# The last expert pair with its down-projection between two halves of an up-projection, and two of the last eight weight transfers issued as sixteen of eight rows

## The reference

```python
logits = jnp.dot(x2, w_router) + b_router        # 320 tokens, 32 experts
top_v, top_e = lax.top_k(logits, TOP_K)          # 4 experts for each token
gate = jax.nn.softmax(top_v, axis=-1)
# for each expert e and its tokens x:
u = x @ w1[e] + b1[e]                            # 1024 -> 2048
x_glu = jnp.minimum(u[..., ::2], 7.0)
x_lin = jnp.clip(u[..., 1::2], -7.0, 7.0)
y = (x_glu * sigmoid(1.702 * x_glu) * (x_lin + 1.0)) @ w2[e] + b2[e]   # 1024 -> 1024
out = h + sum over the token's 4 experts of gate * y
```

## Time and profile before

| | |
|---|---|
| median of 3 runs | 1192.15 us (1191.0 to 1194.05) |
| profiled execution | 1192.19 us |
| its span, first to last instruction | 1190.1 us |
| TensorE clock granted | 0.994 of full speed |
| PE busy | 1149.8 us (97%) |
| DVE, ACT, POOL busy | 367.2, 177.5, 28.9 us |
| DMA | 440.03 MB, 370 GB/s over the span; from 600 us on 423 to 436 in every slice of 30 us but the last |

### The profile page before, as it was taken

One profiled execution on the slowest core, in us unless ns is written; L12 is line 12 of the kernel. 1 busy time (PEld: TensorE's weight loads), 2 busy tenths in 40 slices (PEclk: granted clock), 3 DMA queues, 4 the chain that ended last, 5 costly groups with the idle time before them and its releaser, 6 DMA issues.

```text
span 1190.1 us, 14238 instructions
## 1 busy us (share of the span) xinstructions
PE 1149.8 (97%) x6178; PEld 568.7 (48%) x6178; DVE 367.2 (31%) x759; ACT 177.5 (15%) x327; POOL 28.9 (2%) x54
## 2 busy tenths in 40 slices
PE   8999999999999999999999999999899999999998
PEld 7679988645434343434344343434343434343433
DVE  3637876423312221222223222212121212121222
ACT  2225233022101010111011010101010101010111
POOL 3220000000000000000000000000000000000000
PEclk9999999999999999999999999999999999999999
DMA  9433248967999899999999999999999999999996
GB/s 302 145 90 118 90 150 277 409 256 304 420 425 428 353 439 423 438 425 436 426 435 428 433 429 432 432 427 435 426 436 427 434 429 433 428 433 423 427 428 262
DMA packets 46977, 440.03 MB, mean 370 GB/s; under 512 B 3902, under 2 KB 21664, under 8 KB 29872
## 3 DMA queue, kind: packets, MB, share of 16 engines
q1 hardware_dynamic: 44768, 434.19, 88.0%
q0 software_dynamic: 1904, 4.10, 1.2%
q10 hardware_dynamic: 240, 0.79, 0.2%
HBM read 436.38 MB, written 3.67 MB: 370 GB/s over the span
## 4 chain that ended last, share of the span: by engine, by line
PE 61%; DMA 31%; DVE 4%; ACT 2%; issue 2%; ACTq 0%; DVEq 0%
DMA ring<-in_w 31%; PE ps L1254 22%; PE ps L1312 13%; PE ps L1334 4%; PE ps L793 3%; PE ps L1020 3%; PE ps L1042 2%; PE ps L1119 2%; PE ps L760 2%; PE ps L750 1%; PE ps L727 1%; PE ps L1269 1%; ACT xnT L1692 1%; DMA acc<-in_x_sample 1%; PE ps L1281 1%
## 5 line engine op out<-in xcount | busy, mean ns | idle before, releaser
L1254 PE MATMUL ps<-ring,hnT 128*64 128x512 f32 x2032 | 448.4, 598 | 13.4 <-DMA ring<-in_w 12.7
L1254 PEld LDWEIGHTS ps<-ring,hnT 128*64 128x64 f32 x2032 | 143.6, 138 | 302.2 <-issue 280.7
L1312 PE MATMUL ps<-ring,xnT 128*64 128x512 f32 x992 | 220.8, 597 | 13.8 <-DMA ring<-in_w 13.8
L2226 DVE TENSOR_TENSOR xnT<-ps,b1T 128x512 f32<-128x512 f32 x32 | 22.1, 692 | 448.1 <-PE ps L1269 448.1
L1312 PEld LDWEIGHTS ps<-ring,xnT 128*64 128x64 f32 x992 | 74.9, 138 | 155.3 <-issue 152.4
L1679 ACT COPY hnT<-ps 128x1024 f32<-128x1024 f32 x32 | 32.4, 1012 | 511.9 <-PE ps L1254 511.9
L2247 DVE TENSOR_TENSOR acc<-acc,ps 128x1024 f32<-128x1024 f32 x30 | 36.5, 1218 | 205.0 <-PE ps L1334 187.4
L1334 PE MATMUL ps<-xnT,cst 128*128 128x512 f32 (+1 forms) x180 | 76.0, 619 | 1.6
L1119 PE MATMUL ps<-cst,region 128*128 128x128 f32 x512 | 61.9, 278 | 0.7 <-issue 0.7
L1119 PEld LDWEIGHTS ps<-cst,region 128*128 128x128 f32 x512 | 58.5, 192 | 2.8 <-issue 0.9
L1691 ACT COPY xnT<-ps 64x512 f32<-64x512 f32 x31 | 17.9, 579 | 243.1 <-PE ps L1312 243.1
(11 more groups left out here) (311 smaller groups left out, 840.6 us busy)
## 6 DMA issues: line engine op xcount, KB each, us to landing
ring<-in_w SPq DMA_DIRECT2D x71, 4096.0 KB, 39.1
ring<-in_w SPq DMA_DIRECT2D x33, 2048.0 KB, 26.5
ring<-in_w SPq DMA_DIRECT2D x28, 1024.0 KB, 10.3
ring<-in_w_in SPq DMA_DIRECT2D x17, 1024.0 KB, 5.3
ring<-in_w_o SPq DMA_DIRECT2D x2, 2048.0 KB, 11.7
ring<-in_w SPq DMA_DIRECT2D x8, 512.0 KB, 22.5
ring<-in_w_b SPq DMA_DIRECT2D x1, 2048.0 KB, 11.7
ring<-in_w_a SPq DMA_DIRECT2D x4, 512.0 KB, 6.4
```

The source lines that it names most:

```text
L1254: mm = pe.matmul(ps[o:o + 64, bank + q // 2, into].rearrange("p (j x) -> p j x", x=4), stationary, columns[:, q], start=(at == 0), stop=(a ...
L1312: mm = pe.matmul(ps[64 * c:64 * c + 64, 6, :], hT[:, which, order_of(f), :], ring[:, slot, D * (f % 2) + 512 * c:D * (f % 2) + 512 * c + 512],
L2226: dve.tensor_tensor(glu, ps[:, 2, :].rearrange("p (f t) -> p f t", f=KF), wide(b1T[:, bass.ds(e, 1), 0, :].rearrange("p a f -> p (a f)").u ...
```

## The change

The chunk list of the last pair, PE's order, and ACT's order of two copies are changed together: w1(30) first half, w2(29), w1(30) second half. Transfers 4 and 5 (counted from 0) of the last eight become sixteen each, of eight rows; the same semaphores then count to 256.

```diff
+END_PARTS = [1, 1, 1, 1, 16, 16, 1, 1]
+
 CHUNKS = []
 for _p in range(EXPERTS // 2):
-    CHUNKS += [("w1", 2 * _p, h) for h in range(2)]
-    if _p:
-        CHUNKS += [("w2", 2 * _p - 1, 0)]
+    _up = [("w1", 2 * _p, h) for h in range(2)]
+    if _p == EXPERTS // 2 - 1:
+        CHUNKS += [_up[0], ("w2", 2 * _p - 1, 0), _up[1]]
+    else:
+        CHUNKS += _up + [("w2", 2 * _p - 1, 0)] * (_p > 0)
     CHUNKS += [("w1", 2 * _p + 1, h) for h in range(2)] + [("w2", 2 * _p, 0)]
 CHUNKS += [("w2", EXPERTS - 1, 0)]
...
             def load_end(m, c):
                 for i in range(2):
                     for j in range(2):
-                        sp.dma_start(ring[:, m + i, 1024 * j:1024 * j + 1024].rearrange("p (k c) -> p k c", k=2),
-                                     w2_end[c, i, j]).then_inc(w2_last[4 * c + 2 * i + j], 16)
+                        dst = ring[:, m + i, 1024 * j:1024 * j + 1024].rearrange("p (k c) -> p k c", k=2)
+                        rows_ = P // END_PARTS[4 * c + 2 * i + j]
+                        for r in range(0, P, rows_):
+                            sp.dma_start(dst[r:r + rows_], w2_end[c, i, j][r:r + rows_]).then_inc(w2_last[4 * c + 2 * i + j], 16)
...
                     if f % 2 == 0:
-                        pe.wait_ge(w2_last[4 * c + f // 2], 16 if main else 16 * loads + 16)
+                        n = 16 * END_PARTS[4 * c + f // 2]
+                        pe.wait_ge(w2_last[4 * c + f // 2], n if main else n * loads + n)
...
             def last_body(p, again=None, loads=None, b=None):
                 main = again is None
 
-                up(2 * p, 0, again)
+                up(2 * p, 0, again, steps=range(4))
                 down(2 * p - 1, 1, loads)
+                up(2 * p, 0, again, steps=range(4, KD))
                 turn(2 * p)
...
             def last_body(p):
+                copy_y(2 * p - 1, 1, 3 * p)
                 copy_u(2 * p)
-                copy_y(2 * p - 1, 1, 3 * p)
                 gate_sigmoid(2 * p)
```

## The result

The changed kernel took 1199.46 us (median of four, 1198.41 to 1200.29) against 1192.09 for the one before, measured beside it: a ratio of 1.006, 95% interval 1.0034 to 1.0086. That is +7.4 us; +6.0 was forecast, and the range held it. The profiled execution took 1198.81, its span is 1196.7, so the span grew by 6.6. Where these 6.6 us lie can be read to a tenth. The times compared in this document are of fast executions: one execution of the stepped eight-row kernel took 1482.33 us at a mean granted clock of 0.75, and that kernel's ratio leaves it out.

A forecast was written before the change was run, and what follows sets the result against it. TensorE, busy 97% of the span, was taken as the bound; late issue put the sixth piece at 1183.6 instead of 1177.64, swallowing the order's +1.2: 1192.15 + 6.0 = 1198.2 us, range 1192.6 to 1204.

The forecast's parts named there:

- Part 1: New order of chunks, loads and PE: up's result copy stands bare before the transposes, so up(31) starts 1.2 us later.
- the wait that was to stay: PE's wait for a weight load ending at 1140.36, expected unchanged, now ahead of the last quarter of up(30).
- The +0.4 for this part alone: At the end, the new order alone costs +0.4 us: of its +1.2, small waits for loads absorb the rest.
- Issue: SP issuing 32 small transfers at 0.59 us each: last issued at 1181.5, sixth piece landed at 1183.6.
- Engines: Eight-row transfers use eight engines, so pieces land 2.6 us apart, the sixth at 1180.2, hidden behind 1183.6.
- rival A: In the last loads, issue is cheap and eight engines bind: +2.6, 1194.8 us; 22% together with issues up to 0.5.
- rival B: In the last loads, the partitions' outlet binds, four engines at each: sixth piece at 1194.6, +17, 1209 us; 15%.
- B's objection: Against outlet crowding in the last loads: some engines finish some 5 us ahead, and those on different row blocks don't meet.
- All behind moves as it is: After the wait for the sixth piece, remaining work and stores only shift, by the +6.0 us.
- The sum: PE goes on with the sixth piece at 1183.6 instead of 1177.64, +6.0: 1192.15 + 6.0 = 1198.2 us.
- Its sign that PE goes on before 1181: In the last down-projection: the forecast is wrong if PE goes on with the sixth piece before 1181.
- Rival C: Small transfers hidden on early engines, all issued from 1157.5 on; PE goes on at 1178.0: +0.4, 1192.6 us; 16%.

The follow-up runs named there:

- experiment 1: The new order alone, the eight last transfers whole as in the kernel before: 1192.43 us, ratio 1.0009 to the kernel before.
- e4_rows16: The changed kernel with transfers 4 and 5 as eight transfers of sixteen neighbouring rows each: 1196.28 us, ratio 1.0033 to the kernel before.
- the three fillers: The changed kernel plus three matmuls whose result is never read, ahead of the sixth piece's wait: 1199.51 us, ratio 1.0059 to the kernel before.

## Why the prediction was right, and where it was not

**Part 1: right up to up(31), mis-sized behind it.** The bare copy, the transposes at 1145.2, up(31) at 1152.4 and its disappearance in the wait are all in the trace. One detail differs: PE reached the last part of up(30) later than before, so the wait that was to stay is not in the changed kernel's trace (in that of the order alone it is, 0.96 us); the bare copy began at 1144.17 all the same. The +0.4 for this part alone took idle time of weight loads for time that PE loses: the trace of the order alone has +1.1, as worked out under experiment 1. It cost the forecast nothing, since the longer wait for the sixth piece swallows either.

**Issue: the term was mis-sized, and it isn't the one that binds.** 0.59 us per small transfer came from a single row of ACT's queue. Eight neighbouring rows take 0.30 on SP, one each 0.34 us, and the sixth piece was all issued by about 1175.0, not 1181.5. The queue was read only roughly: the sum had 5.7 of the sixteen out by 1166.6, one each 1.6 us, and the trace has none before 1164.5 and then seven by 1166.6. The runs with stepped rows show that the price exists on SP for another shape, 0.59 with a step. Why the row on ACT had it, with eight neighbouring partitions and no step, no run shows.

**Engines: the reason named as hidden is where the time went.** By the prediction's own sign, issues under 0.46, this is rival A, whose sum was 1175.0 + 2 x 2.6 = 1180.2. Measured is 1177.2 + 5.4 = 1182.6. Its second term is near in size; its first is the step that failed: the fourth piece was taken as untouched. The sixteen engines are not in step. The semaphores of the pieces count an engine's completions, and the traces have the times: those of the fourth piece came from 1168.3 to 1175.0 before, and from 1167.7 to 1177.2 after. With sixteen rows to a transfer (e4_rows16) the first completions of the fifth piece came at 1168.2, while the last of the fourth came at 1177.6. So early engines are already at the small transfers while late ones still carry the whole pieces, and packets are slower just there (87 to 122 ns). That this is rival B's crowding at the outlet of the partitions, at a price of a few microseconds in place of its 17, fits the 64-row kernel and the earlier trace rows but is argued, not shown: no trace tells which engine writes where, and the two kernels with spread rows disagree. B's objection, that engines out of step don't meet, was at most half right; its sign, a wait for the fifth piece as well, is there (0.72).

The engines behind the 5.4 are not settled either: with 64 rows on sixteen engines it is 1182.23 - 1177.37 = 4.9 already (the latter is where PE went on with the fourth piece there), with 32 rows 4.4 (1179.96 - 1175.58). Only the last step, fifth to sixth, is clearly longer with eight rows, 3.6 us in three traces against 2.9 and 2.5 for 64 and 32. How much of that is the eight engines and how much the denser crowding stays open: a transfer of eight neighbouring rows on sixteen engines wasn't tried.

**Not foreseen: the clock.** "All behind moves as it is" was wrong by 1.6 us. A wait of 2.5 us on the critical path cost 4.1.

**The sum.** +6.0 was forecast from a late SP; measured is +5.0 from late engines and +1.6 from the clock. The direction was right. That the size came out near was luck: with issues of 0.34 the prediction's own sums give rival A's +2.6, and the trace has 2.2 more for the late fourth piece, 0.2 for the two behind it and 1.6 for the clock, together 6.6. Two costs that the prediction didn't have took the place of one that wasn't there. Its sign that PE goes on before 1181 if the forecast is wrong was too weak a test, since 1182.6 passes it with another cause; the 0.59 against 0.30 in the issue rows is what tells them apart.

**Rival C** (hidden) fell: the queue did hold SP until 1164.5, and the sixth piece landed 4.6 us behind the 1178 that C needed.

No version that ran beats the kernel before; that nearest to it is the new order alone, which can't be told from it.

## What to carry to other kernels

In every kernel here whose last loads were cut into transfers over some of the partitions, on eight engines or on sixteen, those and the full-width transfers in flight beside them slowed down; where the last loads are within a microsecond of TensorE, leave them at all 128 partitions. Take an issue's price from a row of the same engine and the same access pattern, not from one with the same number of rows. Idle time of weight loads isn't time lost: look whether the matmuls ran on. When a change puts a wait of some microseconds in front of TensorE, look for the lower clock behind it too: it took 1.6 us here.

## What the runs showed of the hardware that was not expected

- SP's issue depends on the pattern as well as on the rows: 0.30 us for eight neighbouring rows, 0.42 for sixteen, 0.43 for 32, 0.61 for 64 (the queue may have held these) and 0.33 for all 128; 0.59 for eight or sixteen rows with a step.
- A run of 2 KB took an engine 87 ns between full-width transfers, 107 with sixteen spread rows, 117 with eight spread rows, 117 to 122 with eight or sixteen neighbouring ones, and 131 to 133 with 32 or 64.
- The sixteen engines of one queue are out of step at the end of a long stream: one piece's completions lie 6.7 us apart in the kernel before (1168.3 to 1175.0 for the fourth).
- The length of one wait doesn't decide the clock: after 2.5 us it fell in all three traces with both pieces in eight neighbouring rows and no fill, and it fell after waits of 0.94 and 1.41 with sixteen rows (0.53 over the next 3.4 us, in which its sixteen instructions took 3.54) and after 1.04 and 0.75 ahead of the three fillers, but not after the 1.77 of the 64-row kernel nor the 1.38 of the 32-row one.
